# A mixture-of-experts decoder step: row norms from TensorE sums, norm weight and row scaling on GpSimd, the first operand split in two steps

## The reference

```python
def _rmsnorm(x, g):
    y = x * lax.rsqrt(jnp.mean(x * x, axis=-1, keepdims=True) + RMS_EPS)
    return y * g

h = h + jnp.concatenate([pool_out, conv_out], axis=-1) @ w_out[l]
hn = _rmsnorm(h, norm2_g[l])
logits = hn @ router_w
top_val, top_idx = lax.top_k(logits, 2)
gates = softmax(top_val)
y = sum over e of combine[:, e] * ((silu(hn @ wg[e]) * (hn @ wu[e])) @ wd[e])
```

## Time and profile before

| what | us |
|---|---|
| median of 3 timed runs | 1567.49 (1567.2 to 1567.58) |
| the profiled execution | 1565.94 |
| its span, first to last instruction | 1564.2 |
| output projection of layer 2 ends (last dense record) | 549.4 |
| first expert pass starts on PE | 570.0 |

### The profile page before, as it was taken

How to read it: one execution, slowest core, us unless ns; L and a number is a source line. 1 busy time by engine, 2 the same in 40 slices (tenths; PEclk the granted TensorE clock), 3 DMA queues, 4 the chain that set the end, 5 groups by cost and what they waited for, 6 DMA issues and landing times.

```text
span 1564.2 us, 21646 instructions
## 1 busy us (share of the span) xinstructions
PE 1516.5 (97%) x7897; PEld 1321.2 (84%) x7897; DVE 1226.7 (78%) x1053; ACT 997.5 (64%) x1018; POOL 155.4 (10%) x209
## 2 busy tenths in 40 slices
PE   7999999999998989999999999999999999999995
PEld 7989999999998977788888888888888888888884
DVE  4797755544498578888888888888888888888887
ACT  5765343333584267777777777777777778777773
POOL 1036200002122237000000000000000000000002
PEclk9999999999999989999999999999999999999998
DMA  6233998343133449999999999999999999999993
GB/s 194 88 129 115 304 303 253 108 142 128 54 115 108 153 171 394 383 366 392 365 364 386 373 363 379 371 369 382 367 363 372 380 367 366 386 359 367 392 367 105
DMA packets 243536, 447.40 MB, mean 286 GB/s; under 512 B 8901, under 2 KB 93957, under 8 KB 243487
## 3 DMA queue, kind: packets, MB, share of 16 engines
q1 hardware_dynamic: 239296, 436.83, 78.4%
q0 software_dynamic: 2960, 9.73, 2.0%
q10 hardware_dynamic: 1231, 0.19, 0.1%
HBM read 421.60 MB, written 25.12 MB: 286 GB/s over the span
## 4 chain that ended last, share of the span: by engine, by line
issue 57%; PE 4%; POOL 3%; DVE 2%; DMA 2%; ACT 1%; DVEq 0%; POOLq 0%; ACTq 0%
PE ps L1571 1%; PE ps L1573 1%; PE ps L1572 1%; POOL og L767 1%; DMA xg<-og,row_i 1%; POOL h L758 1%; POOL xg L734 0%; DMA h<-last_row 0%; DMA last_row<-last_pos 0%; DMA og<-obuf,out_row_i 0%; POOL pick L754 0%; POOL h L726 0%; DVE scratch L1171 0%; DVE y L1173 0%; PE ps L1795 0%
## 5 line engine op out<-in xcount | busy, mean ns | idle before, releaser
L514 DVE TENSOR_TENSOR w_lo<-raw,w_hi 128x2048 fp32r<-128x2048 f32 x336 | 769.5, 2292 | 126.9 <-ACT w_hi L509 125.3
L509 ACT ACTIVATE w_hi<-raw 128x2048 fp32r<-128x2048 f32 x336 | 643.5, 1916 | 133.9 <-PE ps L1573 122.2
L1571 PE MATMUL ps<-w_hi,xg_hi 128*128 128x512 f32 x896 | 354.9, 396 | 2.5 <-DVE xg_lo L1492 1.6
L1572 PE MATMUL ps<-w_lo,xg_hi 128*128 128x512 f32 x896 | 353.6, 395 | 0.0
L1573 PE MATMUL ps<-w_hi,xg_lo 128*128 128x512 f32 x896 | 353.6, 395 | 0.0
L1571 PEld LDWEIGHTS ps<-w_hi,xg_hi 128*128 128x128 f32 x896 | 168.5, 188 | 43.6 <-DVE xg_lo L1492 1.8
L1573 PEld LDWEIGHTS ps<-w_hi,xg_lo 128*128 128x128 f32 x896 | 168.6, 188 | 40.1
L1572 PEld LDWEIGHTS ps<-w_lo,xg_hi 128*128 128x128 f32 x896 | 168.7, 188 | 39.2
L1571 PE MATMUL ps<-x_hi,w_hi 128*128 128x336 f32 x580 | 187.7, 324 | 10.1 <-DVE x_lo L1117 3.8
L1573 PE MATMUL ps<-x_hi,w_lo 128*128 128x336 f32 x580 | 185.5, 320 | 0.0
L1572 PE MATMUL ps<-x_lo,w_hi 128*128 128x336 f32 x580 | 185.2, 319 | 0.0
(11 more groups left out here) (275 smaller groups left out, 1871.2 us busy)
## 6 DMA issues: line engine op xcount, KB each, us to landing
raw<-in_moe_w_gate_dram SPq DMA_DIRECT2D x112, 1024.0 KB, 7.6
raw<-in_moe_w_up_dram SPq DMA_DIRECT2D x112, 1024.0 KB, 7.9
raw<-in_moe_w_down_dram SPq DMA_DIRECT2D x112, 1024.0 KB, 7.5
raw<-in_w_in_dram SPq DMA_DIRECT2D x11, 1024.0 KB, 5.0
raw<-in_ffn_w_gate_dram SPq DMA_DIRECT2D x11, 1024.0 KB, 5.9
raw<-in_ffn_w_up_dram SPq DMA_DIRECT2D x11, 1024.0 KB, 6.4
raw<-in_w_out_dram SPq DMA_DIRECT2D x8, 1024.0 KB, 5.1
obuf<-ones SPq DMA_DIRECT2D x15, 512.0 KB, 7.9
```

What stands on the lines that cost most here:

```text
L509: nc.scalar.activation(hi, r, ACT.Copy).then_inc(hi_done, 1)
L514: nc.vector.tensor_tensor(lo, r, hi.bitcast(F32), ALU.subtract).then_inc(lo_done, 1)
L1571: nc.tensor.matmul(out, a_hi, b_hi, start=start, stop=False)
L1572: nc.tensor.matmul(out, a_hi, b_lo, start=False, stop=False)
```

## The change

- ACT squares each k-tile of `h` as soon as its group is added (eight activations of 128 by 336, into tiles that are free by then). PE multiplies each square, 112 rows at a time, by a column of ones: `token_squares(k)` behind `logits(k)`. The sums come out in the logits' PSUM bank, one column per token tile. The first six k-tiles' products stand behind the fourth, sixth and seventh dense group, those of the last two in the tail.
- ACT's six sums of squares and its three row scalings go. Its Exp table is loaded by a dummy activation ahead of the wait for the gap.
- DVE makes the mean square right after the logits, drops the second half of `hn` and the addition of half sums, and makes the gap behind the selection matrices.
- POOL makes the second half of `hn` and the row scalings `hs`, ahead of the scatter in its queue.
- PE makes five products that nobody reads (`keep_busy`) between the ranks and the gather.
- At the head of each pass ACT and DVE take slot 0, gathered half 0, slot 1, gathered half 1.

The core of the diff:

```diff
@@ POOL
+            pool.wait_ge(gb_landed, 32)
+            for t in range(3):
+                pool.wait_ge(evac, GROUP[("htok", t, 1)] + 1)
+                nc.gpsimd.tensor_tensor(hn[:, t, 512:1024], yt[:, t, 512:1024], gb[:, 0, 512:1024], ALU.mult
+                                        ).then_inc(hn_done, 1)
+            pool.wait_ge(hn_done, 6)
+            pool.wait_ge(token_rstd, 1)
+            for t in range(3):
+                nc.gpsimd.tensor_scalar(hs[:, t, :], hn[:, t, :], nt[0:TT, t, 1:2], None, ALU.mult).then_inc(hn_scaled, 1)
             pool.wait_ge(filled, 16 * (2 * CHUNKS + 1))
@@ ACT, output projection of layer 2
+                    else:
+                        for k in (2 * s, 2 * s + 1):
+                            act.wait_ge(evac, GROUP[("wout", 1, k)] + 1)
+                            nc.scalar.activation(squared(k), h[:, k, :], ACT.Square).then_inc(h_sq, 1)
@@ ACT, routing
-            token_squares(og[:, 0], [(t, 0) for t in range(3)], lambda t, i: act.wait_ge(evac, GROUP[("htok", t, 0)] + 1), hn_sq)
...
-            token_squares(og[:, 0], [(t, 1) for t in range(3)], lambda t, i: act.wait_ge(evac, GROUP[("htok", t, 1)] + 1), hn_sq)
-
+            nc.scalar.activation(table_load[:, 1:2], ones[0:1, 0:1], ACT.Exp)
             act.wait_ge(gap_done, 1)
-            for t in range(3):
-                act.wait_ge(hn_done, 3 + t + 1)
-                nc.scalar.activation(hs[:, t, :], hn[:, t, :], ACT.Copy, scale=nt[0:TT, t, 1:2]).then_inc(hn_scaled, 1)
             nc.scalar.activation(gt[:, :, 1], gt[:, :, 0], ACT.Exp).then_inc(exp_done, 1)
@@ ACT and DVE, head of a pass (DVE the same with gathered_lo)
                 for i in range(ES):
                     split_hi_pass(act, p, i)
-                    if i == 0:
-                        gathered_hi(p)
+                    if i < 2:
+                        gathered_hi(p, i)
@@ DVE, routing
             dve.wait_ge(logits_done, 1)
+            link(nc.vector.tensor_scalar(nt[0:TT, :, 0], SQUARE_SUMS, 1.0 / D, 1e-6, ALU.mult, ALU.add))
...
             dve.wait_ge(hot_done, 2)
-
-            for t in range(3):
-                dve.wait_ge(evac, GROUP[("htok", t, 1)] + 1)
-                nc.vector.tensor_tensor(hn[:, t, 512:1024], yt[:, t, 512:1024], gb[:, 0, 512:1024], ALU.mult
-                                        ).then_inc(hn_done, 1)
-            dve.wait_ge(hn_sq, 6)
-            rstd_tokens()
-            link(nc.vector.tensor_tensor(gt[:, :, 0], top[:, :, 1], top[:, :, 0], ALU.subtract))
-            nc.vector.tensor_tensor(gt[:, :, 0], gt[:, :, 0], nt[0:TT, :, 1], ALU.mult).then_inc(gap_done, 1)
+            rsqrt(nt[0:TT, :, 0], nt[0:TT, :, 1], nt[0:TT, :, 2], nt[0:TT, :, 3])
+            dve.sem_inc(token_rstd, 1)
...
                 nc.vector.tensor_scalar(sel[:, t, :], iota_slot[0:TT, :], pos0[:, t:t + 1], nt[0:TT, t, 1:2],
                                         ALU.is_equal, ALU.mult).then_inc(sel_ready, 1)
+            link(nc.vector.tensor_tensor(gt[:, :, 0], top[:, :, 1], top[:, :, 0], ALU.subtract))
+            nc.vector.tensor_tensor(gt[:, :, 0], gt[:, :, 0], nt[0:TT, :, 1], ALU.mult).then_inc(gap_done, 1)
@@ PE, output projection of layer 2
+                def token_squares(k):
+
+                    pe.wait_ge(h_sq, k + 1)
+                    for t in range(3):
+                        ins = nc.tensor.matmul(SQUARE_SUMS[:, t:t + 1], squared(k)[:, TT * t:TT * (t + 1)],
+                                               ones[:, 0:1], start=False, stop=(k == KD - 1 and t == 2))
+                    return ins
...
                         ins.then_inc(mm_done, 1)
+                        if l == 1 and s and i == (0 if s == 3 else 1):
+                            for k in (2 * s - 2, 2 * s - 1):
+                                logits(k)
+                                token_squares(k)
                     m = 2 * s + 1
-                    if l == 1 and s:
-                        for k in (m - 3, m - 2):
-                            logits(k)
                     if l == 1 and m == KD - 1:
                         logits(KD - 2)
-                        logits(KD - 1).then_inc(logits_done, 1)
+                        logits(KD - 1)
+                        token_squares(KD - 2)
+                        token_squares(KD - 1).then_inc(logits_done, 1)
@@ PE, routing (WARM_ROUTE = 5)
             ins.then_inc(ranks_done, 1)
+            keep_busy(WARM_ROUTE, 6)
```

More of the change, by code:

```diff
@@ L61, in hybrid_trunk @@
     WARM = (12, 10)
+    WARM_ROUTE = 5
     PE_TAPS = (TAPS, TAPS, TAPS - 1)
@@ L257, in hybrid_trunk @@
         eids_f = sb("eids_f", [P, 8], F32, moe)
-        table_load = sb("table_load", [1, 1], F32, moe)
+        table_load = sb("table_load", [1, 2], F32, moe)
         eids = sb("eids", [P, 8], I32, moe)
@@ L262, in hybrid_trunk @@
         SUM_BANK, TOKEN_SUMS = ps[:, 6, 0:T], ps[0:TT, 7, 0:3]
+        SQUARE_SUMS = ps[0:TT, 6, 4 * NE:4 * NE + 3]
         TAP_BANK, N_TAPS = ps[:, 6, 0:L * KC * TAPS], L * KC * TAPS
@@ L296, in hybrid_trunk @@
         state_stored = sem("state_stored")
-        gb_landed, hn_sq = sem("gb_landed"), sem("hn_sq")
+        gb_landed, h_sq, token_rstd = sem("gb_landed"), sem("h_sq"), sem("token_rstd")
         rwg_done, logits_done, hot_done, ranks_done = sem("rwg_done"), sem("logits_done"), sem("hot_done"), sem("ranks_done")
@@ L389, in loads, with squared @@
             return 16 * sum(not is_diag(m) for m in range(n % RAW, n + 1, RAW))
+        def squared(k):
+            return scratch[:, k, :] if k < 4 else y_pool[:, k - 4, :]
         def pooled_at(g):
@@ L1000, in _, with gathered_hi @@
                                      ).then_inc(evac, 1)
-            token_squares(og[:, 0], [(t, 1) for t in range(3)], lambda t, i: act.wait_ge(evac, GROUP[("htok", t, 1)] + 1), hn_sq)
+            nc.scalar.activation(table_load[:, 1:2], ones[0:1, 0:1], ACT.Exp)
             act.wait_ge(gap_done, 1)
-            for t in range(3):
-                act.wait_ge(hn_done, 3 + t + 1)
-                nc.scalar.activation(hs[:, t, :], hn[:, t, :], ACT.Copy, scale=nt[0:TT, t, 1:2]).then_inc(hn_scaled, 1)
             nc.scalar.activation(gt[:, :, 1], gt[:, :, 0], ACT.Exp).then_inc(exp_done, 1)
[L1009 to L1014, removed]
+            def gathered_hi(p, i):
+                act.wait_ge(gather_done, p * 2 + (i + 1))
+                nc.scalar.activation(xg_hi[:, 4 * i:4 * i + 4, :], (X0, X1)[i].rearrange("p (k s) -> p k s", k=4), ACT.Copy
+                                     ).then_inc(xg_hi_done, 1)
             def out_copy(p):
@@ L1037, in after @@
                         out_copy(p)
-                nc.scalar.activation(table_load[:], ones[0:1, 0:1], ACT.Silu)
+                nc.scalar.activation(table_load[:, 0:1], ones[0:1, 0:1], ACT.Silu)
                 for i in range(ES):
                     split_hi_pass(act, p, i)
-                    if i == 0:
-                        gathered_hi(p)
+                    if i < 2:
+                        gathered_hi(p, i)
                     else:
@@ L1487, in _, with gathered_lo @@
             nc.vector.tensor_copy(out_row_i[:], out_row[:]).then_inc(out_rows_done, 1)
[L1489 to L1493, removed]
+            def gathered_lo(p, i):
+                dve.wait_ge(xg_hi_done, p * 2 + (i + 1))
+                nc.vector.tensor_tensor(xg_lo[:, 4 * i:4 * i + 4, :], (X0, X1)[i].rearrange("p (k s) -> p k s", k=4),
+                                        xg_hi[:, 4 * i:4 * i + 4, :].bitcast(F32), ALU.subtract).then_inc(xg_lo_done, 1)
             def hidden(c):
@@ L1513, in expert_pass @@
                     split_lo_pass(dve, p, i)
-                    if i == 0:
-                        gathered_lo(p)
+                    if i < 2:
+                        gathered_lo(p, i)
                     else:
@@ L1603, in spread, with keep_busy @@
                 nc.tensor.matmul(SUM_BANK, ones[0:TT, :], spread_in, start=True, stop=True).then_inc(sums_done, 1)
-            def keep_busy(n):
+            def keep_busy(n, bank=7):
                 for _ in range(n):
-                    nc.tensor.matmul(ps[:, 7, 0:P], ident[:], ones[:], start=True, stop=True)
+                    nc.tensor.matmul(ps[:, bank, 0:P], ident[:], ones[:], start=True, stop=True)
             pe.wait_ge(consts, 1)
@@ L1795, in logits @@
                         ins = nc.tensor.matmul(ps[0:TT, 6, NE * t:NE * (t + 1)], h[:, k, TT * t:TT * (t + 1)],
-                                               rwg[:, k, :], start=(k == 0 and t == 0), stop=(k == KD - 1 and t == 2))
+                                               rwg[:, k, :], start=(k == 0 and t == 0), stop=False)
+                    return ins
[4 more added lines that the diff above has]
+                                               ones[:, 0:1], start=False, stop=(k == KD - 1 and t == 2))
                     return ins
```

## The result

The changed kernel takes 1577.35 us (median of 4 runs, 1573.3 to 1578.79); the kernel before, run beside it, 1567.35 (4 runs, 1566.32 to 1567.58). The ratio is 1.0057, 95% interval 1.0042 to 1.0072: slower by 10.0 us by the medians and by 8.9 by the ratio, where the forecast was 4 us slower and the range ended at 1574.5. The sign came out, the size didn't.

The account below looks back on a forecast made before the run. PE, busy 97% of the span, was taken to bound the kernel. Small records +4.56, DVE's chain -2.85, clock +1.5 and +0.75 gave +3.95 us: 1571.4 us (chance 0.52), range 1567.8 to 1574.5.

Parts of the forecast that it names:

- Part 1: PE in the out-projection: 48 added small records at 0.095 us make MAX8 4.56 us later, bounds 4.37 and 4.85.
- The tail doesn't stall: Tail of the out-projection: PE has 18 records (1.7 us) to do first, so ACT's last square doesn't hold it up.
- The free squares: Rival: one-column products slip in beside dense weight loads at no cost, the 2.85 us gain stays: 1564.6 us; chance 0.08.
- Part 2: ACT in the routing: reaches slot 0 some 5 us earlier and no longer makes DVE wait before slot 1.
- from zero: Counted from the start of DVE's first MAX8 in the routing, at 551.65 us in the profile before.
- Part 3: DVE from MAX8 to the first pass: 2.74 - 0.15 + 0.25, a gain of 2.85 us, bounds 2.6 and 3.1.
- slot 0 on DVE 12.8 us behind MAX8: Sign in DVE's timeline: its first split starts 12.8 us behind MAX8, where it was 15.40.
- The order of the split: Head of each pass: the new order saves 0.25 us in the first pass and zero in the later ones.
- Part 4: GpSimd in the routing: three norm-weight products (1.14 us each), then row scalings; 2.8 us of cover, so no cost.
- The rival that GpSimd becomes the bound: DVE's traffic slows GpSimd's products to 4.1 us each, gather ends 4.9 us past its cover: 1574.1 us; chance 0.06.
- Part 5: Clock in the out-projection: one fall to 1.2 GHz at 1.5 us, a second at even odds, 0.75 us.
- a longer idle time ahead of the first pass: PE idle between gather and first pass: a place where one more clock fall can come, the second at 0.75 us.

Follow-up runs that it names:

- b2: The kernel before with the token squares summed on PE only, the rest of the change left out: 1571.87 us, ratio 1.004.
- a3: The changed kernel with the sums of squares back on ACT and the logits in their old places: 1571.14 us, ratio 1.0027.
- a2: The changed kernel with the second half of hn back on DVE and the row scalings back on ACT: 1570.19 us, ratio 1.0024.
- b3: The kernel before with only the new order of slots and gathered halves at the head of each pass: 1567.92 us, ratio 1.0003.
- a1: The changed kernel with only the three row scalings back on ACT: 1575.85 us, ratio 1.004.
- a4: The changed kernel with 18 products that nobody reads on PE between the gather and the first pass: 1576.24 us, ratio 1.0049.
- c0: The changed kernel itself, run and profiled again: 1577.3 us, ratio 1.0058.
- b4: The kernel before with the first expert's slots 0 and 1 split on ACT and DVE during the out-projection: 1563.04 us, ratio 0.9966.
- b5: b4 with fourteen products that nobody reads added between the ranks and the gather: 1563.92 us, ratio 0.9976 against the kernel before.
- b1: The kernel before with three idle scalings on GpSimd from the hot rows on, whose result nobody reads: 1570.44 us, ratio 1.0025.

## Why the prediction was right or wrong

**Part 1, PE's small records: mechanism right, 0.8 short.** 48 records by 0.095 gave 4.56; MAX8 moved by 5.38, of which 0.20 is the mean-square step that was put ahead of it (the prediction said so, and gave it no price there). The groups ahead of the tail cost what was forecast: 24 records from 526.83 to 529.12, 0.095 each. The tail didn't. Its 24 took 2.79 us (552.13 to 554.92), for 2.27. "The tail doesn't stall" was said of ACT's last square, and for that it holds. But before, 18 logit records had stood ahead of the last k-tile's, and after there are 6, so PE now waits for DVE's last residual addition (list of the weight load's waits):

```profile
PEld ps L1801 <- DVE h L1332: 0.2, 1, 0.2
```

The clock fell at the tail's end as well (0.72 in the window at 554). The free squares, the rival on the other side, are out: b2 and a3 put 5.2 and 5.4 us on them.

**Part 2, ACT: the wait right, the 5 us not.** No wait for ACT stands ahead of DVE's slot 1 any more. But ACT reaches slot 0 only 2.2 us sooner from zero, not 5, since its Exp waits for the gap that DVE, held up, makes late:

```profile
565.98 1.89 ACT L514 ACTIVATE w_hi<-raw 128x2048 fp32r<-128x2048 f32 x1
```

**Part 3, DVE's chain: the sum that came out wrong.** What it lists was right to 0.3 us: without GpSimd's work the chain is 12.5 (a2), for 12.8, and 0.20 of the difference is the mean-square step, which left the chain for the stretch ahead of MAX8. The chain measured 18.33. The missing term is the 5.8 us between, the six held steps (5.76), and the sign "slot 0 on DVE 12.8 us behind MAX8" is the one that didn't come. The order of the split was right: its 0.25 is 0.35 where the first pass is at full clock (6.20 before, 5.85 in a2), and the zero for the later passes fits b3's time.

**Part 4, GpSimd: the step that failed.** The prediction put its work at "2.8 us of cover and costs nothing"; the missing 5.8 us belong in this term. It asked when GpSimd's products are ready, and gave them 2.8 us of cover ahead of their use. Their duration was about right (1.24 us for 1.14). But they don't cost by being late: they cost DVE while they run, and DVE's chain, not the gather, sets the pass. The rival that GpSimd becomes the bound named the right engine and the wrong path: it held GpSimd's products back by DVE's traffic, and dismissed it since "DVE runs only short operations then". Short steps are held too: three of them for nearly the whole of one of GpSimd's products, 1.01 to 1.11 us of 1.24. That rival's 1574.1 came from a gather that ends 4.9 us past its cover; after, the gather ended at 571.64, and the pass still waited 4.9 us for DVE.

The Trainium skill has this rule, in "SBUF — State Buffer", section "Who interferes with whom", and the prediction didn't weigh it: VectorE and GpSimd share a pair of SBUF ports as a lock, and a VectorE instruction with two SBUF inputs, or in one of its two-port modes, waits for a GpSimd instruction that reads SBUF and came first. The trace agrees in part: the held steps take 1.03 to 1.28 us for 0.17, and the three in a row end with GpSimd's products. Three of the six (L1094, L1095, L1467) have two SBUF inputs; the others (L1093, L1446, L1466) have one, and in which mode they ran no run here shows. By the same section of the Trainium skill the lock is held for the whole instruction. Here the row scalings of 2.85 us held a step for 0.9 us and let the subtraction of two SBUF operands at 563.96 pass, so for these the rule isn't borne out, and what released the steps stays open.

**Part 5, the clock: wrong place, and a sum met by luck.** No fall came ahead of the tail, neither after nor in a1, a2, a4, b2 or c0: 24 small records and 20 transposes kept 2.4 GHz, and so did the group before the tail. The rule of the Trainium skill that the prediction quoted on transposes ("TensorE: Matmul & The Clock Gate", Part 4) would have had both groups fall; neither did. The falls were in the tail, in the routing, as before, and, new, in the first pass, after PE had waited for it 4.9 us; in the tail the granted clock was down to 0.72 over the window at 554 already, and the transposes began only at 554.92. The prediction named "a longer idle time ahead of the first pass" as a place for one more fall; it cost 2.3 us (from slot 0 to the second half 8.18 after and 8.12 in c0, for 5.85 in a2 and 5.83 in a4, whose first passes are at full clock), and a2, with 2.3 us of idle time, had none. So the 2.25 us that the forecast put on the clock came, but not for the main reason given, and the idle time was long only by the held steps that it hadn't foreseen: that the two figures agree is luck. One row on which the odds were set was a single execution's, too: layer 0's 24 small records kept the clock in the profile of before, but in eight of the twelve profiles of this case it fell to half within that group (c0, a1, b3, b4) or less than 1 us behind it (a2, a3, a4, b5). Of the changed kernel's own two profiles one kept it and one, c0, didn't (its timeline of PE, then the window at 111):

```profile
108.76 2.60 PE L1774 MATMUL ps<-ones,z 128*112 128x1 f32 x24
```

```profile
111.00:112.00 1.00, 1.00 (x5) 1.00 (x6) 0.42 (x3) 0.00 (x0) 0.00 (x0) 0.50 1.10 347
```

**The sum.** +4.56 became +5.38; -2.85 became +2.58 (2.93 for the chain less 0.35 for the order); the clock's +2.25 became +2.33. From the mark the forecast was +3.96 and the profile shows +10.29; of the 6.33 us between, the second term is 5.43, and it alone changed its sign.

## What to carry to other kernels

Work moved to GpSimd isn't free because GpSimd is idle and its result has cover: list what DVE does while it runs, and if that is a chain of short dependent steps on the path, expect some of them to be held, here by 0.7 to 1.1 us each. A row that shows how long an operation takes doesn't show what it does to its neighbours; an idle copy of it beside the unchanged kernel (b1) shows that in one run. And where an engine's list of waits is nearly empty but for one stretch, first ask what in this stretch could be done ahead of it: splitting two weight slots early took 5.5 us off the kernel before (b4; 4.3 in b5), with nothing moved to another engine. And where a forecast rests on a clock that held or fell in one profile, a second profile of the same kernel can show the other.

## What the runs showed of the hardware that was not expected

- A DVE step on 3 values in each of 112 partitions takes 0.17 us alone; beside a GpSimd elementwise instruction some take 0.88 to 0.90 (b1) or 1.03 to 1.28 (after), and others pass at 0.17. What decides it isn't shown.
- PE's first pass ran at half clock after idle times of 3.0 (b1), 3.1 (b3), 4.2 (a3), 4.9 and 5.0 us (after, c0), and at full clock after 0.8 to 2.3 us (b4, b5, a4, before, b2, a2); in a1, after 2.8, it fell about 1 us into the pass. In b3 a faster gather behind an unchanged DVE chain lengthened that idle time, and the pass began at half clock.
- Idle products that ended 2 us ahead of the gather didn't keep its clock at 2.4 GHz (b5); idle products that ended 1 us ahead of the first pass went with one at full clock (a4).
